# The two output products of a two-block transformer kernel: 16 tiles of 48 matmuls, or seven products of sums per pair of tiles

## What is computed

```
y = g[:, :, 0] * (a @ w_branch_a[layer]) + g[:, :, 1] * (b @ w_branch_b[layer])      # block 1
x = x + y @ w_out[layer]

merged = gate_a * (y_a @ w_proj_a[l]) + gate_b * (y_b @ w_proj_b[l])                 # block 2
y = merged @ w_out[l]
x = x + gate * _rms(y, g_post[l])
```

## Time and profile before

| | us |
|---|---|
| median of 3 runs | 3233.43 (3232.52 to 3235.37) |
| the profiled execution | 3235.39 |
| its span, first to last instruction | 3233.7 |
| product stage of block 1, first to last matmul's start | 1689.95 to 1866.22 |
| product stage of block 2 | 3046.93 to 3224.63 |
| last store issued | 3229.77 |

### The profile page before, as it was taken

The page is one execution under the profiler, slowest core; times in us unless marked ns, Lnnn a source line. Parts: engine busy times, 40 slices in busy tenths (PEclk is TensorE's granted clock), DMA queues, the critical chain, the costliest instruction groups (busy, mean ns, idle before and its releaser), DMA issues. The chain is left out here.

```text
span 3233.7 us, 43574 instructions
## 1 busy us (share of the span) xinstructions
PE 3030.6 (94%) x15436; PEld 2461.9 (76%) x15436; DVE 2020.8 (62%) x3934; ACT 1678.4 (52%) x2700; POOL 1123.7 (35%) x848
## 2 busy tenths in 40 slices
PE   7995999989997899998999979997999999989998
PEld 7994888767885567775778858876887778878787
DVE  7774889989998556555541156667654766443432
ACT  4544679855994667774111033335776577631121
POOL 3451012200221556662222233325555654532232
PEclk9997999999998899999999989998999999999999
DMA  5666433353333631105652245435444544455522
GB/s 172 204 193 199 135 106 89 103 180 112 93 94 126 220 119 48 42 24 165 171 146 102 98 150 151 149 122 194 146 139 146 191 150 127 140 169 154 150 92 91
DMA packets 426561, 436.47 MB, mean 135 GB/s; under 512 B 30976, under 2 KB 320128, under 8 KB 426240
## 3 DMA queue, kind: packets, MB, share of 16 engines
q1 hardware_dynamic: 422672, 426.65, 42.6%
q10 hardware_dynamic: 3696, 7.34, 0.6%
HBM read 277.42 MB, written 156.50 MB: 134 GB/s over the span
## 5 line engine op out<-in xcount | busy, mean ns | idle before, releaser
L1444 PE MATMUL p_pr<-p_hT,p_w_hi 128*128 128x512 f32 x896 | 354.2, 395 | 14.4 <-POOL p_w_lo L1197 9.6
L1445 PE MATMUL p_pr<-p_hT,p_w_hi 128*128 128x512 f32 x896 | 351.9, 393 | 0.0
L1446 PE MATMUL p_pr<-p_hT,p_w_lo 128*128 128x512 f32 x896 | 351.5, 392 | 0.0
L2980 PE MATMUL p_pr<-t2h_high,p_w_hi 128*128 128x512 f32 x784 | 316.0, 403 | 24.0 <-POOL p_w_lo L2729 10.8
L1725 POOL TENSOR_TENSOR a_prob<-a_prob,a_inv 128x1024 f32<-128x1024 f32 (+12 forms) x104 | 250.7, 2419 | 210.1 <-DVE a_inv L1770 209.9
L1197 POOL TENSOR_TENSOR p_w_lo<-p_w_raw,p_w_hi 128x256 fp32r<-128x256 f32 x144 | 107.4, 778 | 601.7 <-DVE p_level L1334 390.9
L2981 PE MATMUL p_pr<-t2h_low,p_w_hi 128*128 128x512 f32 x784 | 308.1, 393 | 0.0
L2982 PE MATMUL p_pr<-t2h_high,p_w_lo 128*128 128x512 f32 x784 | 307.0, 392 | 0.0
L1237 ACT ACTIVATE p_relu<-p_isc,p_level 128x2048 int8<-128x2048 f32 (+5 forms) x192 | 276.9, 1444 | 22.1 <-DVE p_level L1334 17.4
L900 PE MATMUL t_pj_ps<-t_w_hi,t_hT_slot 128*128 128x356 f32 (+2 forms) x768 | 271.6, 354 | 11.7 <-DVE t_w_lo L734 5.5
L1745 DVE CUSTOM_DVE_ANT_0 a_prob<-a_s_ps,a1n_mask 128x512 f32<-128x512 f32 (+3 forms) x320 | 189.4, 608 | 141.5 <-PE a_s_ps L1879 136.9
(11 more groups left out here) (298 smaller groups left out, 7286.0 us busy)
## 6 DMA issues: line engine op xcount, KB each, us to landing
o_gates<-s_gT SPq DMA_DIRECT2D x64, 512.0 KB, 4.9
p_w_raw<-in_w_in SPq DMA_DIRECT2D x56, 512.0 KB, 4.4
t2n_w_raw<-in_w_in SPq DMA_DIRECT2D x56, 512.0 KB, 4.9
s_hT<-t_hT_slot SPq DMA_DIRECT2D x16, 1024.0 KB, 6.4
s_qT<-t_qT_slot SPq DMA_DIRECT2D x32, 512.0 KB, 5.1
p_hT<-s_hT SPq DMA_DIRECT2D x32, 512.0 KB, 9.8
s_gT<-p_o_sb SPq DMA_DIRECT2D x64, 256.0 KB, 4.8
s_gT<-keep_tables SPq DMA_DIRECT2D x64, 256.0 KB, 4.6
```

The source lines that it names most:

```text
L1444: nc.tensor.matmul(pr[n % NPR][:], wh, hi, start=(k == 0), stop=False)
L1445: nc.tensor.matmul(pr[n % NPR][:], wh, lo, start=False, stop=False)
L1446: last = nc.tensor.matmul(pr[n % NPR][:], wl, hi, start=False, stop=(k == KD - 1))
L2980: nc.tensor.matmul(pr[bank][:], wh, hi, start=opens and k == 0, stop=False, skip_group_check=True)
```

## The change

Both product stages are written anew, as products of 2 x 2 blocks with seven products in place of eight. A pair of token tiles gives Y11, Y12 (first tile, first and second half of the 1024 features), Y21, Y22 (second tile); `w_out` gives W11, W12, W21, W22 (halves of rows and columns, each [P, 4, 512]).

- The seven products P1, P5, P6, P2, P7, P3, P4 take Y11, S1, S2, Y12, S4 or S3, Y22, where S3 = Y11 - Y21, S1 = Y21 + Y22, S2 = Y22 - S3, S4 = Y12 - S2, and sums of weights alike. A product is 4 k-slices x 3 = 12 matmuls of 512 columns. The order is P1(0), P5, P6, P2, P3, P7, P1(1), P4(0), P5(1) and so on: a pair's P4 stands behind the next pair's P1. 56 products per block.
- Each pair uses three of six PSUM banks. P1, P5 and P2 begin a bank. ScalarE copies P1, P5 and P6 out of theirs (`keep`) before P6, P3 and P7 go on adding to them; VectorE adds a bank to a kept quarter after P2, P3 and P7 (`add`).
- `yT` leaves SBUF. VectorE writes each unit's sum to `y_out` (two places), SyncE stores it in DRAM (`s_yT`), and `load_y(p)` fetches the four blocks of a pair (256 KB each), pair 0 beside the last group of units, pair 1 behind the last unit's store.
- Per pair, VectorE makes the four sums (`sum_y`, 128x512 each), ScalarE seven high parts (`high_y`), GpSimd seven low parts (`low_y`), all 128x512. In GpSimd's queue the statistics of a pair's two tiles stand behind the whole `low_y` of the next pair.
- Weights: VectorE makes the sums of blocks, six operations of 128x2048 among the last units and two low blocks besides (P2, P3); GpSimd makes the low blocks of P1, P5, P6, P7 and P4.
- `x_in` shrinks to one place, [P, 1024], and a tile's `x` is loaded when the tile before is finished.
- `w_raw`, `w_hi` and `w_lo` are laid out by output chunk; what they hold in the branch stage stays the same.

The diff, cut to its core. `finish_at(n)` is the point of the order, counted in products, at which tile n is finished.

```diff
-        return sb("w_raw", [P, KD, D], F32), sb("in_raw", [P, RING, BANK], F32)
+        return sb("w_raw", [P, KD, KD, P], F32), sb("in_raw", [P, RING, BANK], F32)
...
+def product_order(pairs):
+    P1, P5, P6, P2, P7, P3, P4 = range(7)
+    sequence = []
+    for p in range(pairs):
+        sequence += [(p, P1)] + ([(p - 1, P4)] if p else []) + [(p, x) for x in (P5, P6, P2, P3, P7)]
+    sequence.append((pairs - 1, P4))
+    return sequence, {product: q for q, product in enumerate(sequence)}
...
+    def start(p):
+        return 7 * p - 1
+    def finish_at(n):
+        p, i = divmod(n, 2)
+        return AT[p, P4 if i else P3] + (3 if second else 1 if i else 2)
...
+            def load_wo():
+                if not second:
+                    sp.wait_ge(mixed, GROUPS * KB)
+                for n, r in enumerate((r11, r12, r22, r21)):
+                    k, j = (0, 0, 1, 1)[n], (0, 1, 1, 0)[n]
+                    sp.dma_start(r[:], wo[0, k * KB * P:(k + 1) * KB * P, j * BANK:(j + 1) * BANK].rearrange("(k p) n -> p k n", p=P)
+                                 ).then_inc(wo_loaded[n], 16)
...
+            def store_y(u):
+                tg, dc = divmod(u, KD)
+                sp.wait_ge(summed, u + 1)
+                sp.dma_start(c.yT[dc, :, tg * BANK:(tg + 1) * BANK], y_out[:, u % 2]).then_inc(y_stored[u % 2], 16)
+            def load_y(p):
+                s = p % 2
+                for b, k0, i in ((Y11, 0, 0), (S1, 0, 1), (Y22, KB, 1), (Y12, KB, 0)):
+                    t0 = (2 * p + i) * P
+                    sp.dma_start(y_raw[s][b], c.yT[k0:k0 + KB, :, t0:t0 + P].rearrange("k p t -> p k t")).then_inc(y_loaded[s], 16)
+            def load_x(n):
+                sp.dma_start(x_in, x_dram[rows(n), :]).then_inc(x_loaded, 16)
...
+                store_y(u)
+                if u == LAST - 1:
+                    load_wo()
+                if u == LAST + 1:
+                    sp.wait_ge(weighed, LAST)
+                    for s in (0, 1):
+                        sp.wait_ge(y_stored[s], 16 * KD // 2)
+                    load_y(0)
+            sp.wait_ge(weighed, UNITS_ALL)
             for s in (0, 1):
-                sp.wait_ge(stored[s], 16 * T // 2)
+                sp.wait_ge(y_stored[s], 16 * UNITS_ALL // 2)
+            load_y(1)
+            load_x(0)
+            for q in range(N + 6):
+                for n in range(T):
+                    if q == finish_at(n) + 1:
+                        p, i = divmod(n, 2)
+                        sp.wait_ge(out_done, n + 1)
+                        if n + 1 < T:
+                            load_x(n + 1)
+                        sp.dma_start(out_dram[rows(n), :], x_out(p, i)).then_inc(stored[2 * (p % 2) + i], 16)
+                for p in range(2, PAIRS):
+                    if q == start(p - 1) + 2:
+                        sp.wait_ge(product_done, AT[p - 2, P4] + 1)
+                        load_y(p)
...
+            def low_y(p):
+                s = p % 2
+                for n, b in enumerate(NEEDED):
+                    pool.wait_ge(y_hi_done[s], 7 * (p // 2) + n + 1)
+                    nc.gpsimd.tensor_tensor(y_lo[s][b], y_raw[s][b], f32(y_hi[s][b]), ALU.subtract).then_inc(y_lo_done[s], 1)
+            low_block(P1)
+            low_y(0)
+            for b in (P5, P6, P7, P4):
+                low_block(b)
+            for p in range(1, PAIRS + 1):
+                if p < PAIRS:
+                    low_y(p)
+                for t in (2 * p - 2, 2 * p - 1) if second else ():
...
+            def high_y(p):
+                s = p % 2
+                act.wait_ge(y_summed, p + 1)
+                for b in NEEDED:
+                    nc.scalar.activation(y_hi[s][b], y_raw[s][b], ACT.Copy).then_inc(y_hi_done[s], 1)
+            def keep(p, x):
+                i = x // 2
+                act.wait_ge(product_done, AT[p, {X11: P1, X22: P5, X12: P6}[x]] + 1)
+                if p == 0:
+                    act.wait_ge(summed, UNITS_ALL)
+                elif p == 1:
+                    for s in (0, 1):
+                        act.wait_ge(y_stored[s], 16 * UNITS_ALL // 2)
                 else:
...
+                    act.wait_ge(stored[2 * (p % 2) + i], 16 * (p // 2))
+                nc.scalar.activation(quarter(p, x), banks(p)[1 if x == X22 else 0], ACT.Copy).then_inc(kept, 1)
+            def square(n):
+                p, i = divmod(n, 2)
+                if i:
+                    act.wait_ge(product_done, AT[p, P4] + 1)
+                    nc.scalar.activation(quarter(p, X21), banks(p)[0], ACT.Copy).then_inc(taken, 1)
+                    act.wait_ge(taken, p + 1)
+                act.wait_ge(added, 3 * p + 2 + i)
+                if n >= 2:
+                    act.wait_ge(out_done, n - 1)
+                nc.scalar.activation(b_ps[3][:].rearrange("p j n -> p (j n)"), x_out(p, i), ACT.Square, scale=D ** -0.5,
+                                     accum_out=stat[:, i, 0:1]).then_inc(squared, 1)
...
+            high_block(P1)
+            high_y(0)
+            for b, n in ((P5, 1), (P6, 2)):
+                act.wait_ge(wo_summed, n)
+                high_block(b)
...
+            for q in range(N + 3):
+                for x, pos in ((X11, P1), (X22, P5), (X12, P6)):
+                    for p in range(PAIRS):
+                        if q == AT[p, pos] + 1:
+                            keep(p, x)
+                if q == 1:
+                    act.wait_ge(wo_summed, 3)
+                    high_block(P7)
+                if q == 2:
+                    act.wait_ge(wo_lo_done[P3], 1)
+                    high_block(P4)
                 if second:
-                                         accum_out=stat[:, t % 2, 0:1]).then_inc(squared, 1)
+                    for p in range(PAIRS):
+                        if q == AT[p, P3] + 2:
+                            square(2 * p)
+                        if q == AT[p, P4] + 1:
+                            square(2 * p + 1)
+                for p in range(1, PAIRS):
+                    if q == start(p - 1) + 4:
+                        high_y(p)
...
+            def sum_y(p):
+                s = p % 2
+                y = y_raw[s]
+                dve.wait_ge(y_loaded[s], 64 * (p // 2 + 1))
+                step(nc.vector.tensor_tensor(y[S3], y[Y11], y[S1], ALU.subtract))
+                nc.vector.tensor_tensor(y[S1], y[S1], y[Y22], ALU.add)
+                step(nc.vector.tensor_tensor(y[S2], y[Y22], y[S3], ALU.subtract))
+                nc.vector.tensor_tensor(y[S4], y[Y12], y[S2], ALU.subtract).then_inc(y_summed, 1)
+            def sum_first():
+                dve.wait_ge(weighed, LAST + 2)
+                for n in (0, 1):
+                    dve.wait_ge(wo_loaded[n], 16)
+                nc.vector.tensor_tensor(WEIGHTS_RAW[P5], r12[:], r11[:], ALU.subtract).then_inc(wo_summed, 1)
+            def sum_second():
+                dve.wait_ge(weighed, LAST + 4)
+                dve.wait_ge(wo_loaded[2], 16)
+                step(nc.vector.tensor_tensor(WEIGHTS_RAW[P6], r22[:], r12[:], ALU.subtract))
+                nc.vector.tensor_tensor(WEIGHTS_RAW[P6], WEIGHTS_RAW[P6], r11[:], ALU.add).then_inc(wo_summed, 1)
+                dve.wait_ge(wo_summed, 2)
+                step(nc.vector.tensor_tensor(r12[:], r22[:], r12[:], ALU.subtract))
+            def sum_last():
+                dve.wait_ge(wo_lo_done[P2], 1)
+                step(nc.vector.tensor_tensor(r21[:], r21[:], r12[:], ALU.subtract))
+                dve.wait_ge(wo_lo_done[P1], 1)
+                nc.vector.tensor_tensor(r21[:], r21[:], r11[:], ALU.subtract).then_inc(wo_summed, 1)
...
+            def add(p, x):
+                dve.wait_ge(product_done, AT[p, {X11: P2, X12: P3, X22: P7}[x]] + 1)
+                dve.wait_ge(kept, 3 * p + {X11: 1, X22: 2, X12: 3}[x])
+                bank = banks(p)[{X11: 2, X12: 1, X22: 0}[x]]
+                nc.vector.tensor_tensor(quarter(p, x), bank, quarter(p, x), ALU.add).then_inc(added, 1)
+            def finish(n):
+                p, i = divmod(n, 2)
+                o = x_out(p, i)
+                dve.wait_ge(x_loaded, 16 * (n + 1))
+                if second:
+                    dve.wait_ge(powered, n + 1)
+                    nc.vector.scalar_tensor_tensor(out=o, in0=o, scalar=stat[:, i, 2:3], in1=c.gpost_gate[:],
+                                                   op0=ALU.mult, op1=ALU.mult).then_inc(scaled, 1)
+                    dve.wait_ge(scaled, n + 1)
...
+                if u >= 2:
+                    dve.wait_ge(y_stored[u % 2], 16 * (u // 2))
+                nc.vector.tensor_tensor(y_out[:, u % 2], gates[:, u % 2, 0], gates[:, u % 2, 1], ALU.add).then_inc(summed, 1)
...
+                if u == LAST + 2:
+                    sum_y(0)
+                if u == LAST + 3:
+                    sum_first()
+                if u == LAST + 4:
+                    sum_second()
+                if u == LAST + 6:
+                    low_block(P2)
+                    sum_last()
```

(35 more changed lines are left out.)

## The result

The changed kernel took **3275.12 us**, the median of 4 runs (3271.04 to 3280.06), against 3234.08 us for the kernel before on the same chip: 1.0128 times as long, 95% interval 1.011 to 1.0145, or 41.0 us more. The forecast was 3285 us, range 3250 to 3315. The profiled execution of the changed kernel took 3274.44 us with a span of 3272.7 us, against 3235.39 and 3233.7 us before.

A forecast was written before the change was run, and what follows sets the result against it. TensorE's matmuls were taken to bound both product stages. Terms -43.6 - 5.6 + 33.6 + 52.4 + 5.2 + 2.2 + 5.9 + 1.6 gave +51.7 us, so 3285 us on the median of 3233.4, range 3250 to 3315.

The forecast's parts named there:

- The ring of block 2: Block 2 pairs: a cycle of waits through GpSimd, VectorE and SyncE lasts 24.7 us against 19.05 of matmuls; +33.6 us.
- The change of stage: Branch to products, each block: queued VectorE and GpSimd work delays P6 by 20.7 us, pair 1's P1 by 5.4; +52.4 in all.
- The sign that the forecast gave: At the change of stage, VectorE's 2048-column operations would read 4 us and more instead of 2.3.
- Matmuls, -43.6: Both product stages: 192 matmuls fewer at 0.227 us each, -43.6 us.
- Clock in block 1, +1.6: Block 1, behind pair 1's wait: the slow clock costs 1.6 us where matmuls bound afterwards.
- Gates: Branch stages: gates of units 26 and 27 queue behind loads; 1.5 us in block 1, 3.7 in block 2, +5.2.
- Last P4: End of each product stage: the last P4 waits 1.1 us for the last add, twice, +2.2.
- The end of block 1: Behind block 1's products: last tile's x is loaded only after its neighbour is finished, +2.5 us.
- The end of block 2: Behind block 2's products: last tile's late x load, plus a copy and an add, +3.4 us.
- B: Rival: block 2's cycle binds but the change of stage is cheap, 2 x 11.4 in place of 52.4; 3255 us, chance 0.14.
- C: Rival: all dearer, cycle 27.7 us, changes of stage 31 each, slow clock every cycle; 3323 us, half 3304; chance 0.14.
- D: Rival: block 2's cycle closes under 19.05 us; 3217 us (chance 0.07), or 3251 with dear changes of stage (0.03).

The follow-up runs named there:

- The three orders: Changed kernel with y loads ahead of x load and store: 3267.41 us; with sums ahead of finish: 3284.61 us; with both moves: 3241.40 us.
- the copy's experiment: Changed kernel with ScalarE's copy of the first pair's first quarter in a free place, not waiting for the last unit's sum: 3272.32 us, 1.0126 times before.
- on its own: Seven products in block 1 only, block 2's output stage as in the kernel before: 3233.35 us, 0.9996 times before.
- both orders: Changed kernel with y loads ahead of x load and store, and next pair's sums ahead of the odd tile's finish: 3241.40 us, 1.0028 times before.
- the same edit: Free place for ScalarE's copy: on changed kernel 3272.32 us; with both orders and low blocks on VectorE 3235.10; with shortened change of stage 3205.28, without it 3215.56.
- the kernel with the loads first: Changed kernel with SyncE issuing the next pair's y loads ahead of the x load and the store: 3267.41 us, 1.0112 times before.
- the kernel with both cures and the free place: Changed kernel with both orders and low blocks of P5, P6, P7, P4 on VectorE (3231.36 us), plus the free place for ScalarE's copy: 3235.10 us, 1.0007.

## Why the forecast held, point by point

**The ring of block 2: right.** 24.4 us a pair for 24.7, by every step named. The three orders (23.3, 25.6 and TensorE's own pace) show that it is a ring of two queues and not a price of GpSimd's low parts, which are the same in all of them. The waits of pairs 2 to 7 are only 2.0 to 5.2 us each, 22.5 us in all, and not the forecast 33.6, since the slow clock behind a wait lengthens the next matmuls and so eats part of the following wait: between 3116 and 3119 us the granted clock is 0.50, the lower level of 1.2 GHz. Matmuls at less than the usual pace hold the other 9.7 us of the 32.2 by which the six cycles exceed 19.04. That term was rightly not added a second time.

**The change of stage: right in kind, too dear.** The last unit's sum ended at +22.5 us (forecast +25.4), P6 started at +23.3 (26.2) and P1 of pair 1 at +39.0 (42.4) in both blocks: 3.4 us too much per block, which is the miss of the product stages (+1.4 for +5.0, +32.2 for +35.6) but for 0.2 us. VectorE beside GpSimd, block 2, by the timeline of VectorE:

```profile
3046.29 3.38 DVE L2379 TENSOR_TENSOR r_w_raw<-o_r 128x2048 f32<-128x2048 f32 x1
3049.70 3.26 DVE L2380 TENSOR_TENSOR r_w_raw<-r_w_raw,o_r 128x2048 f32<-128x2048 f32 x1
3052.99 3.27 DVE L2382 TENSOR_TENSOR o_r<-o_r 128x2048 f32<-128x2048 f32 x1
...
3057.56 3.63 DVE L2495 TENSOR_TENSOR o_y_out<-o_gates 128x512 f32<-128x512 f32 x1
...
3062.36 3.82 DVE L2495 TENSOR_TENSOR o_y_out<-o_gates 128x512 f32<-128x512 f32 x1
3066.10 2.28 DVE L2359 TENSOR_TENSOR o_w_lo<-o_r,o_w_hi 128x2048 fp32r<-128x2048 f32 x1
```

and by the timeline of GpSimd:

```profile
3038.20 7.55 POOL L2246 TENSOR_TENSOR o_in_lo<-r_in_raw,o_in_hi 128x512 fp32r<-128x512 f32 x4 [11.91 <-ACT o_in_hi L2271]
...
3054.08 11.55 POOL L2235 TENSOR_TENSOR o_w_lo<-r_w_raw,o_w_hi 128x2048 fp32r<-128x2048 f32 x2
```

Two 512-column adds took 3.63 and 3.82 us while GpSimd made its two 2048-column parts, and the 2048-column operation behind them, with GpSimd idle, 2.28. Together with three 2048-column operations at 3.3 to 3.4 us for 2.29, VectorE lost 9.1 us from unit 28's multiply to the last sum, where 11.1 were forecast. (A fourth such operation, at 3039.95, stands ahead of that multiply, and a wait of 1.09 us follows it.) The sign that the forecast gave, 4 us and more for these operations, was not met: one low part of y holds them up and not a block. The direction of the earlier trace rows held; what the walk did not have is that GpSimd pays as well: 1.89 us for each of four low parts that the earlier trace rows give as 1.27, and 5.8 for each block for 4.63. The rule of the Trainium skill (SBUF — State Buffer, Terms) that the two engines block each other for whole instructions fits these rows.

**What the forecast did not see:** which wait of the change of stage was the dear one. It gave 20.7 us to P6 and 5.4 to P1 of pair 1. By the copy's experiment on the changed kernel P6's wait was worth nothing by itself, since P1 of pair 1 came no earlier without it. The forecast had the chain that decides: from the last unit's sum over its store (landed at +24.9, forecast 28.2), the loads of pair 1's y (+31.0, forecast 33.8) and VectorE's first sum, held up by GpSimd's P4 block (3.77 us for 0.69), to P1. It runs past P6 and has 16.5 us behind the last sum, 17.0 by the forecast:

```profile
3074.92 2.34 DMA s_yT<-o_y_out
...
3079.30 4.08 DMA r_in_raw<-s_yT
3083.40 3.77 DVE r_in_raw L2365
```

So the delay of 22.7 us at P1 of pair 1 belongs to the time of the last sum and to this chain. GpSimd's P7 and P4 blocks come in by the 3.1 us of that first sum.

**Matmuls, -43.6: right**, by block 1's pairs at 19.04 us each. **Clock in block 1, +1.6: right**, 20.76 us for the pair behind the wait, 1.7 over 19.04. The 0.52 that the forecast read in the earlier trace rows for the time after the 7.5 us wait is of a window that begins 2.8 us before the wait ends; from 1493 to 1496 the clock is 0.50. **Gates: +2.2 and +4.2** for 1.5 and 3.7, with new waits of TensorE for VectorE's multiply of 1.91 and 3.39 us, 13.5 us ahead of the last branch matmul. **Last P4:** waits of 0.79 and 0.78 us for 1.1. **The end of block 1:** TensorE's next instruction starts 14.1 us behind the last output matmul's start where it was 12.0, +2.2 for +2.5; in the ten other kernels with the new stage in block 1 it is 14.4 to 14.8. **The end of block 2:** +1.4 for +3.4, since the x load is issued at 3261.98, while the last product still runs.

**Block 1 was forecast at +9.0 us** and cost -1.3 (-4.5 to +1.6) on its own; block 2 at +42.7, and what is left to it is some 42. The part of the miss in block 1 that is not the change of stage lies in the stretch behind it, which reads 3.3 us less where 2.5 more was due, although its first wait did become 2.2 us longer: the rest of it, which nobody changed, reads 5.5 us less. No experiment touched that rest. The whole stretch reads 996.8 to 1001.3 us in the ten other profiles, and the front of the kernel, which nobody changed either, 1488.5 to 1494.2; before's 1001.9 is a single reading at the upper end. So whether the 5.5 us are a gain or scatter stays open. They are about half of the 10 us by which the forecast lies above the measured time.

**Rivals.** B (cheap change of stage) would have shown P6 waiting under 3 us: it waited 10. C's cycle of 27.7 us and its changes of stage of 31 did not come, nor did its uncovered slow clock. D's ring under 19.05 us is what both orders produce, and with dear changes of stage it was put at 3251: the kernel with both orders is 3241.

## What to carry to other kernels

Follow who waits for whom around one turn of the loop, through every queue: a load of the next turn that stands behind the end of this turn, on any queue, closes a ring, and its length, not an engine's busy share, is the pace. Opening it needs every queue at once; half of the cure can cost time. And the longest wait in a list says nothing of what its removal is worth, before the next wait behind it is known, and what that one waits for: the same edit was worth nothing in one kernel, nothing or a small loss in a second, and 10 to 14 us in a third. Where several waits hang on one event, here the last unit's sum, that event is the place to work on.

## What the runs showed of the hardware beyond that

A wait of TensorE can cost more than itself. After the 5.48 us wait at 3060.74 nine matmuls took 3.87 us, where 2.04 is their pace of 0.227 us: 1.8 us more; after the 10.17 us wait at 3075.64 fifteen took 6.25 us for 3.4, 2.9 more. The granted clock is 0.50, the lower level, in the 3 us from 3061 and from 3076. After the waits of 1.79 and 2.00 us the pace is the usual one and the clock 1.00 (3091.5 to 3094.5 and 3188.6 to 3191.6).

What the first matmul reads does not tell which it will be. Behind the 3.19 us wait at 3237.85 it reads 0.47 us, as at the full clock, but the clock falls right behind it (0.59 in 3238 to 3241) and 1.7 us are lost. Nor does a wait's length alone, under 3 us: in the kernel with the loads first a wait of 1.94 us at 3090.18 cost 1.7 us (clock 0.50 in 3090.5 to 3093.5), and one of 2.47 us at 3207.81 nothing (1.00 in 3208 to 3211). In all eleven traces with the new stage every wait of over 3 us in the product stages was followed by a slow stretch, which cost 1.1 to 3.0 us.

Such a cost counts where no later wait takes it up. In block 2 of the kernel with both cures and the free place, three waits of together 13.3 us were followed by 6.2 us of loss, where the one wait of 14.8 us that they replaced was followed by 2.6.
